# A hybrid decoder layer on one core: the solves of the delta rule one and three units earlier, a third decay buffer, and the sample products spread over the rows of a dense product

## What is computed

```python
xn = rmsnorm(h, norm_mix); z = xn @ w_in                      # 1024 -> 3592
y_a = z_B * causal_dwconv(z_C * z_H)                          # short convolution, 3 taps
q, k, v = silu(causal_dwconv(z_QKV))                          # 4 taps; q, k l2-normed per head
g, beta = -exp(a_log) * softplus(z_A + dt_bias), sigmoid(z_BETA)
# gated delta rule, per head and chunk:
decay = exp(G_i - G_j), i >= j                                # G = cumsum(g)
lower = strict((beta * k) @ k.T * decay)
u, w = triangular_solve(eye + lower, [v * beta, k * beta * exp(G)])
v_new = u - w @ S;  o = (q * exp(G)) @ S + (q @ k.T * decay) @ v_new
S = S * exp(g_last) + (k * exp(g_last - G)).T @ v_new
h += concat(y_a, rmsnorm(o) * silu(gate)) @ w_out
h += relu(rmsnorm(h) @ w_up) ** 2 @ w_down;  y = rmsnorm(h)
```

## Time and profile before

| | |
|---|---|
| median of three runs | 1356.91 us |
| the profiled execution | 1354.47 us |
| its span, first to last instruction | 1352.6 us |
| busy: PE, weight loads, DVE, ACT, POOL | 98%, 96%, 62%, 30%, 40% |
| mean granted TensorE clock | 0.994 |

### The profile page before, as it was taken

The page is one execution under the profiler, slowest core; times in us unless marked ns, Lnnn a source line. Parts: engine busy times, 40 slices in busy tenths (PEclk is TensorE's granted clock), DMA queues, the critical chain, the costliest instruction groups (busy, mean ns, idle before and its releaser), DMA issues.

```text
span 1352.6 us, 22490 instructions
## 1 busy us (share of the span) xinstructions
PE 1323.2 (98%) x9025; PEld 1291.9 (96%) x9025; DVE 836.0 (62%) x1400; ACT 410.5 (30%) x805; POOL 536.9 (40%) x550
## 2 busy tenths in 40 slices
PE   6999999999999999999999999999999999999997
PEld 4899999789999999999999999999999999999997
DVE  4466689633654646556685666666667567566855
ACT  6566552111212222232132222322222223223312
POOL 2332123211212211122267467574674765746811
PEclk9999998899999999999999999999999999999999
DMA  6123553643323223321111112112112121111212
GB/s 190 38 69 101 147 151 106 150 130 93 94 79 79 67 67 88 96 80 32 47 42 53 47 33 62 47 48 63 31 49 61 32 64 47 48 48 45 68 43 116
DMA packets 161850, 99.88 MB, mean 74 GB/s; under 512 B 19639, under 2 KB 156371, under 8 KB 161746
## 3 DMA queue, kind: packets, MB, share of 16 engines
q1 hardware_dynamic: 137216, 85.31, 21.7%
q10 hardware_dynamic: 24530, 13.13, 3.6%
HBM read 77.62 MB, written 20.80 MB: 73 GB/s over the span
## 4 chain that ended last, share of the span: by engine, by line
PE 85%; DVE 7%; DMA 2%; ACT 2%; issue 1%; POOL 1%; SPq 1%; DVEq 0%; ACTq 0%; POOLq 0%
PE banks L1820 9%; PE banks L1822 9%; PE banks L1821 9%; PE banks L1337 8%; PE banks L1339 8%; PE banks L1338 8%; PE banks L1839 7%; PE banks L1840 7%; PE banks L1838 7%; DVE inverse L2142 2%; DVE outer L2140 2%; PE banks L1854 1%; PE banks L1855 1%; PE banks L1856 1%; PE banks L1519 1%
## 5 line engine op out<-in xcount | busy, mean ns | idle before, releaser
L1820 PE MATMUL banks<-hg_high,w_high 128*128 128x384 f32 (+1 forms) x768 | 249.5, 325 | 0.5 <-POOL w_low L905 0.5
L1822 PE MATMUL banks<-hg_high,w_low 128*128 128x384 f32 (+1 forms) x768 | 247.6, 322 | 0.0
L1821 PE MATMUL banks<-hg_low,w_high 128*128 128x384 f32 (+1 forms) x768 | 247.3, 322 | 0.0
L2492 DVE TENSOR_TENSOR hT<-hT,banks 128x528 f32<-128x528 f32 x280 | 189.5, 701 | 84.3 <-PE banks L1840 75.6
L1337 PE MATMUL banks<-xn_high,w_high 128*128 128x384 f32 (+1 forms) x672 | 229.4, 341 | 0.1
L1338 PE MATMUL banks<-xn_low,w_high 128*128 128x384 f32 (+1 forms) x672 | 221.2, 329 | 0.0
L1339 PE MATMUL banks<-xn_high,w_low 128*128 128x384 f32 (+1 forms) x672 | 221.0, 329 | 0.0
L773 POOL TENSOR_TENSOR w_low<-w_raw,w_high 128x1024 fp32r<-128x1024 f32 x37 | 91.5, 2473 | 262.7 <-ACT w_high L981 262.7
L1820 PEld LDWEIGHTS banks<-hg_high,w_high 128*128 128x128 f32 x768 | 144.2, 188 | 2.5 <-POOL w_low L905 2.3
L1821 PEld LDWEIGHTS banks<-hg_low,w_high 128*128 128x128 f32 x768 | 144.3, 188 | 0.1
L1822 PEld LDWEIGHTS banks<-hg_high,w_low 128*128 128x128 f32 x768 | 144.2, 188 | 0.0
(11 more groups left out here) (315 smaller groups left out, 2778.5 us busy)
## 6 DMA issues: line engine op xcount, KB each, us to landing
w_raw<-in_w_up SPq DMA_DIRECT2D x32, 512.0 KB, 4.0
w_pair<-in_w_down SPq DMA_DIRECT2D x32, 512.0 KB, 3.4
w_raw<-in_w_in SPq DMA_DIRECT2D x28, 512.0 KB, 4.4
w_raw<-in_w_out SPq DMA_DIRECT2D x8, 512.0 KB, 4.1
x_slice<-in_x_prompt SPq DMA_DIRECT2D x8, 512.0 KB, 4.1
out<-y_tok SPq DMA_DIRECT2D x8, 512.0 KB, 2.7
x_tok<-in_x_prompt SPq DMA_DIRECT2D x2, 1536.0 KB, 14.7
v_kept_rows<-v_feat SPq DMA_DIRECT2D x4, 536.0 KB, 3.3
```

The source lines that it names most:

```text
L1820: pe.matmul(bank[:, 0:w], w_h[half][:, k, :], hg_h[:, k, c0:c0 + w], start=(k == 0), stop=False)
L1821: pe.matmul(bank[:, 0:w], w_h[half][:, k, :], hg_l[:, k, c0:c0 + w], start=False, stop=False)
L1822: ins = pe.matmul(bank[:, 0:w], w_l[half][:, k, :], hg_h[:, k, c0:c0 + w], start=False, stop=(k == KT - 1))
L2492: dve.tensor_tensor(hc, hc, both, ALU.add if sign > 0 else ALU.subtract).then_inc(acc_read_dve, 1)
```

## The change

1. The small solve runs behind units 25 and 26 instead of 28 and 29, and SP stores its result at unit 28 instead of 29.
2. The decay blocks lie in three buffers, `Dm[t % 3]`, with three semaphores `d_sent`. `decay_diff(t)` waits, from t = 4 on, for the store of tile t - 3 and for `keep_at(t - 3)`. ACT's first write of a gate row, which reuses the memory, waits for all three.
3. The wide solve runs behind units 29 to 37 instead of 30 to 38, and SP's two stores stand at unit 37.
4. The sample products go between the rows of the products of units 36 and 37: behind each of the 16 rows of depth (3 matmuls), 2 of them. The wait for `w_kept` so stands behind the first row of unit 36 instead of its last.

The instructions of GpSimd, the low parts of the weights among them, are the same in the same order. No engine has another amount of work.

```diff
-        Dm = [place(f"decay{i}", [P, NH * P], F32, RG + i * HB) for i in range(2)]
+        Dm = [place(f"decay{i}", [P, NH * P], F32, RG + a * HB) for i, a in enumerate((0, 1, 4))]
...
-        SMALL_SOLVE = (28, 29)
-        SOLVE = {30: 3, 31: 3, 32: 3, 33: 3, 34: 3, 35: 3, 36: 5, 37: 5, 38: 3}
+        SMALL_SOLVE, SMALL_SENT = (25, 26), 28
+        SOLVE = {29: 3, 30: 3, 31: 3, 32: 3, 33: 3, 34: 3, 35: 3, 36: 5, 37: 5}
...
             def spill_decay(t):
                 sp.wait_ge(d_exp, t + 1)
-                sp.dma_start(D_d[t - 1], Dm[t % 2][:, :]).then_inc(d_sent[t % 2], 16)
+                sp.dma_start(D_d[t - 1], Dm[t % 3][:, :]).then_inc(d_sent[t % 3], 16)
...
-                if u == SMALL_SOLVE[-1]:
+                if u == SMALL_SENT:
...
-            def sample_products(half):
+            def sample_products(part):
...
-                n = NH * NSEQ // 2
-                for i in range(n * half, n * half + n):
+                n = NH * NSEQ // (2 * KT)
+                for i in range(n * part, n * part + n):
...
-                if u in TILE0["sample"]:
-                    sample_products(TILE0["sample"].index(u))
...
-                        dense_part(n, g, normed, range(KT))
+                        if u in TILE0["sample"]:
+                            for k in range(KT):
+                                dense_part(n, g, normed, [k])
+                                sample_products(KT * TILE0["sample"].index(u) + k)
+                        else:
+                            dense_part(n, g, normed, range(KT))
...
             def decay_diff(t):
...
-                if t >= 3:
-                    dve.wait_ge(d_sent[t % 2], 16 * ((t - 1) // 2))
-                    dve.wait_ge(kk_kept, t - 1)
+                if t >= 4:
+                    dve.wait_ge(d_sent[t % 3], 16 * ((t - 1) // 3))
+                    dve.wait_ge(kk_kept, t - 2)
```

More of the change, by code:

```diff
@@ L308, in build @@
         g_rows = sem("g_rows"); g_diff = sem("g_diff"); d_exp = sem("d_exp"); kk_made = sem("kk_made"); kk_kept = sem("kk_kept")
-        d_sent = [sem("d_sent0"), sem("d_sent1")]; at_sent = [sem("at_sent0"), sem("at_sent1")]
+        d_sent = [sem("d_sent0"), sem("d_sent1"), sem("d_sent2")]; at_sent = [sem("at_sent0"), sem("at_sent1")]
         gathered = sem("gathered"); gathered0 = sem("gathered0"); inverse_set = sem("inverse_set")
@@ L1079, in evict @@
                     if i == 0 and g == 0:
+                        for b in range(3):
+                            act.wait_ge(d_sent[b], 16 * ((NT - 1 - (b - 1) % 3 + 2) // 3))
                         for b in range(2):
-                            act.wait_ge(d_sent[b], 16 * (NT // 2))
                             act.wait_ge(at_sent[b], 16 * (NT // 2 + 1 - b))
@@ L1105, in decay_exp @@
             def decay_exp(t):
-                c, d = rows(t), Dm[t % 2] if t else qk0
+                c, d = rows(t), Dm[t % 3] if t else qk0
                 act.wait_ge(g_diff, t + 1)
@@ L1122, in load_decay @@
             def load_decay(t):
-                act.wait_ge(d_sent[t % 2], 16 * ((t + 1) // 2))
+                act.wait_ge(d_sent[t % 3], 16 * ((t + 2) // 3))
                 act.dma_start(qk[:, :], D_d[t - 1]).then_inc(d_load, 16)
@@ L1605, in sample_products @@
                                     start=True, stop=True)
-                if half:
+                if part == 2 * KT - 1:
                     ins.then_inc(sample_made, 1)
@@ L2129, in keep_at @@
                     dve.wait_ge(at_sent[t % 2], 16 * (t // 2))
-                scaled_product(At_s[t % 2], ps[5], p_, Dm[t % 2] if t else qk0, rows(t), t).then_inc(kk_kept, 1)
+                scaled_product(At_s[t % 2], ps[5], p_, Dm[t % 3] if t else qk0, rows(t), t).then_inc(kk_kept, 1)
             def solve_step(tb, inv, tmp, size, j):
```

## The result

The changed kernel takes **1360.97 us** (median of 7 runs, 1358.75 to 1363.45), the one before 1355.92 us beside it (7 runs, 1352.38 to 1359.62): a ratio of 1.0033, 95% interval 1.0019 to 1.0047. It is about 5 us slower, where I forecast 1350.3 us, and lies above the range.

The account below looks back on a forecast made before the run. PE, busy 98% of the span, was taken as the bound, with gains only where it stands or runs slowly. 1.0 + 0.6 + 1.9 - 0.6 + 2.3 + 0.4 = 5.6 us off 1355.8 gave 1350.3 us, range 1345 to 1356.5.

Parts of the forecast that it names:

- The wait for w: Unit 36: PE wants w 4.4 us sooner, DVE is 4 us ahead; -0.6 us (bounds 0 and -4.4).
- my signs: Signs of being right, among them `keep_w0` about 211 us with a PE wait under 1.5 us.
- Rival 3: DVE's queue delays `keep_w0`, PE stands 3.7 us in unit 36: 1355.8 us or slower, 6%.
- The clock falling inside the mixed rows: Sign of being wrong: a fall of PE's clock within the mixed rows of units 36 and 37.
- The sample products: Units 36 and 37: 3.2 us of clock regained, 1.3 us paid for mixing; net +1.9 us (bounds -1.3 and +1.9).
- the eighth slice: Clock row, one of two slices spanning 203 to 271 us; behind it, what is gained before is kept.
- rival 1: The clock isn't held or the falls had another cause; gain 2.4 us, 1353.4 us, chance 20%.
- The decay buffers and the small solve: PE's waits for the decay of tile 7 (+1.0 us) and for DVE's copy (+0.6 us) both end.
- The wide solve's stores: Earlier stores shorten PE's wait for the tile loop's first load: +2.3 us (bounds 1.4 and 3.2).
- the fall at 253.0 us: Clock fall behind tile 0's small products: expected to stay, counted as nothing.
- The last fall: Clock fall from 262.6 us, behind the 2.5 us hole: 1.7 us, taken as +0.4 us (bounds 0 and 1.7).
- What SP's two stores push back: SP's queue: the delayed v rows, last columns and a gate row are wanted only at unit 48 or later.

Follow-up runs that it names:

- the kernel with w at 34: Changed kernel with w made behind unit 34 instead of 35, mixing left as it is: 1354.08 us, ratio 0.9982 against the kernel before.
- the twins: Changed kernel with w behind unit 34 and SP storing the last v rows before the wide solve's blocks, mixed against bursts: 1347.92 and 1348.04 us.
- the version with bursts and w at 34: Changed kernel with sample products in two bursts of 16, w behind unit 34, v rows stored before the wide solve's blocks: 1348.04 us, ratio 0.9933.
- unit 37 plain: Changed kernel with sample products mixed into units 36 and 38, w still behind unit 35: 1354.09 us, ratio 0.9985 against the kernel before.
- the one with the v rows first: Changed kernel with w behind unit 34 and SP storing the last v rows before the wide solve's two blocks: 1347.12 us, again 1347.92 us.
- the kernel with bursts: Changed kernel without its mixing, sample products in two runs of 16 behind units 36 and 37: 1353.72 us, ratio 0.9979 against the kernel before.

## Why the prediction was wrong

**The wait for w: the step that failed.** Its premises held: DVE stood 2.6 us for the gather (I took 4), its tap ended 3.5 us sooner (I took 4), `keep_w0` ended at 211.46 ("about 211 us"). PE wanted w 2.4 us sooner by what it had gained in front, not 1.6, and so stood 1.94 us instead of 0.6, above the 1.5 us of my signs. That miss of 1.3 us is small. What failed is the price per us of wait: I charged the idle time alone, -0.6 us (bounds 0 and -4.4). The wait ends in front of fifteen more mixed rows, which keep the clock where it fell. Against the kernel with w at 34, the first pair comes 2.62 us behind the start of its unit instead of 0.50 (2.1 us), from there to the end of unit 37 it is 26.64 us instead of 14.18 (12.5 us: rows of 1.61 and 1.81 us against 0.86 and 0.97), and from there to `turn_v0` 9.33 instead of 7.72 (1.6 us). Together they are the 38.59 - 22.40 = 16.2 us of the table. Rival 3 named the very wait ("PE stands ... in the first rows of unit 36"), but charged 1.6 us of clock behind it, one fall as in the old trace, and gave it 6%. I had asked whether mixed rows hold 2.4 GHz and never whether they would bring it back from 1.2. "The clock falling inside the mixed rows" was close, but it fell in front of them.

**The sample products.** With w there in time the clock is held, as I took it from unit 0. I sized the stretch's gain at 1.9 us (3.2 less 1.3 for mixing), and between the twins it is 3.1. A mixed unit of 384 columns takes 7.77 us, a plain one and its burst 4.3 + 3.5 us, so the price of mixing, 14 x 0.09 us, isn't there. The first wide matmul behind a pair does take 0.26 us, as I said, but the pair itself takes 0.36 us instead of 4 x 0.109 (0.109 us is one pass of a sample product, and not a whole one as I wrote):

```profile
217.99 0.51 PE L1605 MATMUL banks<-wq_sample,S_sample 128*128 128x8 f32 x4
218.35 0.42 PE L1338 MATMUL banks<-xn_high,w_high 128*128 128x384 f32 x1
218.61 0.34 PE L1339 MATMUL banks<-xn_low,w_high 128*128 128x384 f32 x1
```

The 3.2 us of clock were read from one execution: by the other profiles with bursts it is 1.7 to 6.8 us. And I counted the gain as kept, since "PE works almost without a wait" behind the eighth slice. That was true of slices further on, not of the next two units: no end gain can be measured.

**The clock at the bursts and at the waits.** The clock falls in two ways here: with PE busy all the time, in or just behind a burst (0.57 from 216 to 220 us in the version with bursts and w at 34), and around a wait with mixed rows behind it: 1.5 us into a wait of 1.94 us in the changed kernel, 0.4 us behind the end of one of 1.92 us with unit 37 plain. The rule of the Trainium skill that I weighed (TensorE: Matmul & The Clock Gate, HAM oscillation — how this bites in real kernels), no idle gaps of some length, says nothing of the first kind and points at the second, though the gap here is shorter than the one that it warns of; I set it aside for both. The same page (The HAM clock gate) says that what the chip judges by runs free of the kernel's start. The traces agree, without proving it. The kernel with w at 34 has the same wait of 0.94 us at L1616 and the same products behind it as the one with the v rows first, yet its clock stayed at 1.00 there. And of ten bursts of the same 32 passes two lost no clock at all; rival 1 said as much of other executions of the kernel before. It fits too that the kernel before spreads over 6.6 to 9.7 us on its three chips (23 to 29 executions), the one with bursts over 9.0 (twelve), and mixed ones over 2.7 to 5.5 (ten to twelve).

**The decay buffers and the small solve.** Predicted 1.0 + 0.6; both waits went, as said. The third buffer alone brings PE 2.3 us sooner to unit 36 and to `turn_v0`. It ended the wait for DVE's copy too, without the small solve moved, so the 0.6 us weren't the solve's. Of the 0.7 us beyond the two waits, PE has 0.3 already at unit 3, before anything of the change runs; between units 24 and 27, where the decay's wait of 1.0 us was, it gains 1.4 us, and between units 33 and 36, where that of 0.6 us was, 0.7.

**The wide solve's stores.** Right in what it said of L1519, which no longer waits: 2.5 us, where the sum had 2.3. The rest of the 4.1 us up to the tile loop is the fall at 253.0 us. I had it stay, since it "hangs on products that don't change", but the same products ran at 1.00 in the changed kernel. The last fall is gone too, 1.7 us for the 0.4 of the sum. Two parts were wrong. X was stored at 244.61 us, not before 240, for PE and DVE ran late (241.25 us with w at 34). And "What SP's two stores push back ... is wanted at unit 48 or later" missed `keep_v(0)` at unit 40, which overwrites what the pushed store still reads. In the changed kernel this costs nothing, since it is late; with w at 34 it was worth 6 to 7 us more, on top of the 6.9 us of w itself.

Of the whole: 2.4 us gained in front (1.6 predicted), 12.7 lost in the stretch (1.3 gain predicted), 4.1 gained up to the tile loop (2.3 predicted) and 1.9 behind its start (0.4 predicted). Outside the stretch all came out better than predicted; the sign of the change is that of the wait for w alone.

## What to carry to other kernels

Price a wait by what PE does behind it, not by its length: 2 us of standing cost 16 us here, because the mixed rows behind it kept TensorE at the level of its clock that they found, while 1.6 us of standing in front of a dense unit cost no clock. Before work is spread through a product, its operand must be there with a margin, since the first piece is wanted at once. And when a store is moved up in an in-order queue, look for who may not overwrite until the stores that it now passes are done. Last, a fall of the clock that one profile shows may be missing in the next execution: what it is worth takes several.

## What the runs showed of the hardware

- Mixed rows keep the level of the clock that they find: rows of three matmuls (304 or 384 columns) and 4 records of 8 columns hold 1.00 over 14.7 us, and hold 0.50 over 26 us (212 to 238 us) though PE is 100% busy. Dense rows brought 2.4 GHz back within one unit each time.
- A burst of 3.5 us of nothing but 8-column passes, PE 100% busy, was cut or followed by a fall in eight of ten cases, and held 1.00 in the other two (the first in the kernel with bursts, the second in that with the third buffer).
- Rows of wide matmuls and pairs of 8-column products cost no more than their parts (0.97 us a row against 3 x 0.17 + 4 x 0.109): the first wide matmul takes 0.26 us instead of 0.17, as behind a burst, but the pair 0.36 instead of 0.44.
- Local gains left no trace in the time that could be measured: 22.4 us against 25.5 us in one stretch, 1347.9 against 1348.0 us in the medians. A stretch of a trace shows where time is saved, not that it is.
